# First layer's attention: the projections of heads 2 to 7 as seven products per head pair, with their sums on VectorE

## What is computed

```python
ql, kl, vl, ... = in_proj_split(h_l @ w_in)      # 256 latent tokens
qc, kc, vc, ... = in_proj_split(h_c @ w_in)      # 256 context tokens
# per head: q, k are 2 x 64 wide, v is 128 wide; rope on the latent q, k
def diff_attend(q, k, v, lam):
    s = jnp.einsum('bqhcd,bkhcd->bchqk', q, k).astype(jnp.float32) * (ATT_HEAD_DIM ** -0.5)
    p = jax.nn.softmax(s, axis=-1)
    a = p[:, 0] - lam * p[:, 1]
    return jnp.einsum('bhqk,bkhe->bqhe', a.astype(v.dtype), v)
o_l = diff_attend(ql, concat(kl, kc), concat(vl, vc), lam)
o_c = diff_attend(qc, kc, vc, lam)               # first layer only
```

## Time and profile before

| | us |
|---|---|
| median of 3 runs | 2659.3 |
| lowest, highest | 2656.21, 2660.04 |
| span of the profiled execution | 2653.7 |
| TensorE busy | 2620.1 (99%) |
| VectorE, ScalarE, GpSimd busy | 1544.2, 780.3, 1083.9 |

### The profile page before, as it was taken

One profiled execution on the slowest core, in us unless ns is written; L12 is line 12 of the kernel. 1 busy time (PEld: TensorE's weight loads), 2 busy tenths in 40 slices (PEclk: granted clock), 3 DMA queues, 4 the chain that ended last, 5 costly groups with the idle time before them and its releaser, 6 DMA issues.

```text
span 2653.7 us, 39393 instructions
## 1 busy us (share of the span) xinstructions
PE 2620.1 (99%) x15122; PEld 2004.0 (76%) x15122; DVE 1544.2 (58%) x2600; ACT 780.3 (29%) x1786; POOL 1083.9 (41%) x874
## 2 busy tenths in 40 slices
PE   8999999999999999999999999999999999999998
PEld 7779994555555666788878888876666677899998
DVE  1537835777778334797859760226766733566253
ACT  2430113565665333100021110013554522201210
POOL 4018971232323112274425554411221222586885
PEclk9999999999999999999999999999999999999999
DMA  9337666434432220244455532264444321287653
GB/s 284 97 112 213 180 200 168 111 96 106 106 99 72 56 54 26 72 113 129 123 159 160 162 91 88 87 183 117 111 108 107 96 72 50 79 224 216 172 167 120
DMA packets 519018, 330.96 MB, mean 125 GB/s; under 512 B 15296, under 2 KB 485680, under 8 KB 518832
## 3 DMA queue, kind: packets, MB, share of 16 engines
q1 hardware_dynamic: 507600, 296.10, 39.6%
q0 software_dynamic: 10784, 31.46, 4.8%
q10 hardware_dynamic: 448, 0.89, 0.1%
HBM read 327.06 MB, written 1.34 MB: 124 GB/s over the span
## 4 chain that ended last, share of the span: by engine, by line
PE 90%; DVE 3%; issue 2%; ACT 1%; DVEq 1%; POOL 1%; PEld 1%; PEldq 0%; DMA 0%; POOLq 0%; ACTq 0%
PE ps L1736 42%; PE ps L1373 23%; PE ps L1903 3%; PE ps L1915 3%; PE ps L1894 3%; PE ps L1878 2%; PE ps L1855 1%; PE ps L2017 1%; PE ps L2053 1%; PE ps L2040 1%; PE ps L2116 1%; POOL TMP L844 1%; PE ps L1693 1%; PE ps L2029 0%; PE ps L1841 0%
## 5 line engine op out<-in xcount | busy, mean ns | idle before, releaser
L1373 PE MATMUL ps<-xnT,W 128*128 128x512 f32 (+1 forms) x1760 | 650.2, 525 | 2.2 <-DVE TMP L2583 0.8
L1373 PEld LDWEIGHTS ps<-xnT,W 128*128 128x128 f32 x1760 | 329.8, 190 | 290.3 <-issue 260.1
L1736 PE MATMUL ps<-TMP,W 128*128 128x128 f32 (+1 forms) x2840 | 481.9, 320 | 3.6 <-DVE TMP L2450 2.8
L1736 PEld LDWEIGHTS ps<-TMP,W 128*128 128x128 f32 x2840 | 422.5, 192 | 35.9 <-issue 3.7
L1736 PE MATMUL ps<-BIG,W 128*128 128x128 f32 (+1 forms) x2744 | 438.6, 314 | 0.0
L819 POOL TENSOR_TENSOR W<-W 128x512 f32<-128x512 f32 x137 | 188.8, 1378 | 560.6 <-DMA W<-in_w_mlp 246.0
L1736 PEld LDWEIGHTS ps<-BIG,W 128*128 128x128 f32 x2744 | 393.1, 191 | 27.5 <-issue 1.2
L1736 PE MATMUL ps<-xnT,W 128*128 128x128 f32 (+1 forms) x2032 | 324.2, 311 | 0.0
L1736 PEld LDWEIGHTS ps<-xnT,W 128*128 128x128 f32 x2032 | 288.7, 191 | 18.9 <-issue 0.8
L905 ACT ACTIVATE TMP<-ps 128x512 f32<-128x512 f32 (+3 forms) x229 | 104.9, 465 | 653.5 <-PE ps L1736 394.5
L2208 DVE SCALAR_TENSOR_TENSOR TMP<-W,cact,TMP 128x512 f32<-128x512 f32 x168 | 205.8, 1258 | 7.9
(11 more groups left out here) (349 smaller groups left out, 3139.9 us busy)
## 6 DMA issues: line engine op xcount, KB each, us to landing
W<-in_w_in SPq DMA_DIRECT2D x188, 512.0 KB, 4.1
W<-in_w_mlp SPq DMA_DIRECT2D x128, 512.0 KB, 4.0
W<-in_ada_w SPq DMA_DIRECT2D x96, 512.0 KB, 4.0
BIG<-cs_rows POOLq DMA_DIRECT2D x96, 256.0 KB, 4.7
W<-in_w_ssd_o SPq DMA_DIRECT2D x32, 512.0 KB, 5.1
W<-in_w_gate SPq DMA_DIRECT2D x22, 512.0 KB, 6.1
W<-in_w_up SPq DMA_DIRECT2D x22, 512.0 KB, 4.5
W<-in_w_down SPq DMA_DIRECT2D x16, 512.0 KB, 3.6
```

Source lines behind the costliest of these rows:

```text
L1373: last = mm(dst, w[:, c, 0:m], rhs(k), start=k == 0, stop=k == total - 1)
L1736: done = mm(PS[bank][:, third + half * H:third + half * H + H], w[:, at + c, :], x[:, c, :], start=first and opens and c == 0, stop=last a ...
```

## The change

Heads 0 and 1 stay as they are. Heads 2 to 7 of the first layer are taken in three pairs, and each of q, k, v of a pair is a *job* (nine in all). A job multiplies the two heads' weights (two blocks of output columns), split in halves of the depth (4 chunks each), with the tokens, split by depth and by latent and context (256 each). This is a 2 x 2 by 2 x 2 block product, and it is done in seven block products (steps 1 to 7) in place of eight. Its sums are:

- of tokens, t1 to t4, once, by VectorE in units 0 to 3 (1024 elements each);
- of weights, four additions of 128x512 per job by VectorE, into two extra slots of the ring (`attsums`), spread over units 1 to 20 by the table `WEIGHT_SUMS`;
- of results: step 1 opens bank 4 and ScalarE copies it; steps 6, 7 and 4 add onto the same bank, and ScalarE copies after each (256 columns). Bank 5 takes step 2, is opened again by step 5, and step 3 adds onto it; VectorE adds bank 5 to the copied blocks after steps 2, 7 and 3. Each next step on a bank waits for that copy or addition.

A step is 4 matmuls of 256 columns (q, k) or 8 of 128 (v). `SEVEN_FILL` places the 63 steps in the slots of units 4 to 24; `GATE_FILL` places 12 gate matmuls in units 24 to 31. ScalarE makes the copy of part 0 ahead of the unit's exponentials if part 0 has exactly one step, and behind them otherwise. The token sums for the merge move to units 25 to 28. Odd pairs keep q, k and v in `qkB`, `vaB0`, `vaB1`, in space that the attention's output uses later. Rope of head 2 in unit 7 needs all four copies of the key job.

```diff
+SEVEN_JOBS = [(0, p, t) for p in (1, 2, 3) for t in "qkv"]
+SEVEN_AT = {1: 4, 2: 8, 3: 16}
+SEVEN_FILL[1] = [["q1 q2", "q6 q5", "q7"], ["q4 q3", "k1 k2", "k6 k5"], ["k7", "", "k4 k3"], ["v1 v2", "v6 v5", "v7"],
+                 ["v4 v3", "", ""]]
+SEVEN_FILL[2] = [["", "q1", "q2"], ["q6", "q5", "q7"], ["", "q4", "q3"], ["k1", "k2", "k6"], ["k5", "k7", ""],
+                 ["k4", "k3", "v1"], ["v2", "v6", "v5"], ["v7", "", "v4"], ["v3", "", ""]]
+SEVEN_FILL[3] = SEVEN_FILL[2]
+GATE_FILL = {24: (0, 1, 0), 25: (1, 1, 0), 26: (1, 1, 0), 27: (1, 0, 0), 28: (1, 1, 0), 29: (1, 0, 0), 30: (1, 1, 0),
+             31: (1, 0, 0)}
+WEIGHT_SUMS = {s: n for s, n in enumerate((0, 1, 1, 2, 2, 1, 2, 2, 1, 1, 2, 1, 1, 1, 1, 1, 1, 1, 2, 1, 2))}
...
+                def seven_copied(s, part):
+                    for job, step in seven_of(s, part) if l == 0 else ():
+                        if step in (1, 6, 7, 4):
+                            seven_done(act, job, step)
...
+                            A(seven_out(job, i, m), PS[4][:, 0:S], ACT.Copy, scale=scale).then_inc(c_cp, 1)
...
                 for s, (h, qt, k0, nk) in enumerate(us):
                     b = 2 * (s % 2)
+                    one = l == 0 and len(seven_of(s, 0)) == 1
+                    if one:
+                        seven_copied(s, 0)
                     act.wait_ge(u_mx["att"], 32 * l + s + 1)
...
+                    if not one:
+                        seven_copied(s, 0)
                     if s:
                         prob_t(s - 1)
+                    seven_copied(s, 1)
...
+                    if step == 1:
...
+                            pe.wait_ge(c_cp, 4 * job)
...
+                    elif step == 2:
+                        if job:
+                            pe.wait_ge(c_ad, 3 * job)
...
+                    elif step == 6:
+                        pe.wait_ge(c_ws, job + 1)
+                        pe.wait_ge(c_t, 2)
+                        pe.wait_ge(c_cp, 4 * job + 1)
...
+                    elif step == 5:
+                        pe.wait_ge(c_ad, 3 * job + 1)
...
+                    elif step == 7:
+                        pe.wait_ge(c_t, 4)
+                        pe.wait_ge(c_cp, 4 * job + 2)
...
+                    elif step == 4:
+                        pe.wait_ge(c_cp, 4 * job + 3)
...
+                    else:
+                        pe.wait_ge(c_ad, 3 * job + 2)
...
                     for n, t in enumerate(("ga", "gs")):
-                        pe.wait_ge(kept["att"], 24 * l + 24)
...
+                            pe.wait_ge(c_cp, 4 * len(SEVEN_JOBS))
+                            pe.wait_ge(c_ad, 3 * len(SEVEN_JOBS))
...
+                    if s:
+                        seven_added(s - 1, 2)
                     if h < 7 and qt == nq - 1 and l == 0:
+                        dve.drain()
                         rope(h + 1)
...
+                    seven_added(s, 0)
+                    seven_added(s, 1)
                     if s:
                         out_of(s - 1)
+                    if l == 0 and s < 4:
+                        next(seven_sums, None)
+                    for _ in range(WEIGHT_SUMS.get(s, 0) if l == 0 else 0):
+                        next(seven_weights, None)
-                    if (4 if l else 20) <= s < (16 if l else 24):
+                    if (4 if l else 25) <= s < (16 if l else 29):
                         next(first_token_sums, None)
```

More of the change, by code:

```diff
@@ L522, in build @@
         va = [va0, va1]
+        qkB, vaB0, vaB1 = carve(BIG[:, 8192:], (2, 2, T), (4, P), (4, P))
         fr, = carve(TMP[:, 1536:], (4, T))
@@ L595, in build @@
         out_t, out_d = sem("out_transposed"), sem("out_stored")
+        c_pe, c_cp, c_ad, c_ws, c_t = (
+            sem(f"seven_{x}") for x in ("products", "copied", "added", "weights_summed", "tokens_summed"))
         q_s, q_v, q_t, q_p1, q_p2, q_p7, q_rel = (
@@ L654, in slot_of, with weights_ready @@
             return W[:, number[key] % SLOTS, :, :]
-        def quick_weights(eng, j):
-            *pair, k1, k2 = quick_keys(j)
+        def weights_ready(eng, keys):
+            *pair, k1, k2 = keys
             for key in pair:
@@ L696, in flat, with seven_keys, paired, job_for @@
             return v.rearrange("p a b -> p (a b)")
+        def seven_keys(job):
+            l, p, t = SEVEN_JOBS[job]
+            return [("att", l, 2 * p, t), ("att", l, 2 * p + 1, t), ("attsums", l, p, t, 0), ("attsums", l, p, t, 1)]
+        def paired(l, h):
+            return l == 0 and h >= 2
+        def job_for(h, t):
+            return SEVEN_JOBS.index((0, h // 2, t))
+        def qk_of(l, h):
+            return (qkB if paired(l, h) and h // 2 % 2 else qk)[:, h % 2, :, :]
+        def va_of(l, h):
+            return ((vaB0, vaB1) if paired(l, h) and h // 2 % 2 else va)[h % 2]
+        def seven_done(eng, job, step):
+            if step in (1, 2, 7):
+                eng.wait_ge(c_pe, 3 * job + (1, 2, 7).index(step) + 1)
+            else:
+                made(eng, seven_keys(job)[{6: 0, 4: 1, 5: 2, 3: 3}[step]])
+        def seven_out(job, i, m):
+            l, p, t = SEVEN_JOBS[job]
+            whole = flat(va_of(l, 2 * p + i)) if t == "v" else qk_of(l, 2 * p + i)[:, "qk".index(t), :]
+            return whole[:, m * S:(m + 1) * S]
         def by_half(v):
@@ new lines, in _, with filled @@
+                many = 12 // (3 * nq)
+                def filled(s, part):
+                    h = us[s][0]
+                    if l == 0 and h:
+                        for job, step in seven_of(s, part):
+                            product_of(job, step)
+                        n = GATE_FILL.get(s, (0, 0, 0))[part]
+                    else:
+                        n = many if h < 7 else (8 // nq, 4 // nq, 0)[part]
+                    for _ in range(n):
+                        next(ahead, None)
@@ L2059, in _ @@
                 for s, (h, qt, k0, nk) in enumerate(us):
-                    if qt == 0:
+                    if qt == 0 and (l or h == 0):
                         ahead = pieces(h + 1) if h < 7 else gate_pieces(0)
+                    if l == 0 and s == min(GATE_FILL):
+                        ahead = gate_pieces(0)
                     scores(s)
-                    for _ in range(many if h < 7 else 8 // nq):
-                        next(ahead, None)
+                    filled(s, 0)
                     if s:
@@ new lines, in _, with seven_added @@
+                seven_sums, seven_weights = sums_for_seven(), weights_for_seven()
+                def seven_added(s, part):
+                    for job, step in seven_of(s, part) if l == 0 else ():
+                        if step not in (2, 7, 3):
+                            continue
+                        seven_done(dve, job, step)
+                        dve.wait_ge(c_cp, 4 * job + {2: 1, 7: 3, 3: 2}[step])
+                        i, m = {2: (0, 0), 7: (1, 1), 3: (0, 1)}[step]
+                        part_of = PS[5][:, 0:S]
+                        whole = seven_out(job, i, m)
+                        if SEVEN_JOBS[job][2] == "q":
+                            V.scalar_tensor_tensor(out=whole, in0=part_of, scalar=HD ** -0.5, in1=whole,
+                                                   op0=ALU.mult, op1=ALU.add).then_inc(c_ad, 1)
+                        else:
+                            V.tensor_tensor(whole, part_of, whole, ALU.add).then_inc(c_ad, 1)
```

142 lines of the change are left out of this document (112 added, 30 removed).

## The result

| | before | after |
|---|---|---|
| median, us | 2659.61 (4 runs) | 2673.64 (4 runs) |
| lowest, highest | 2656.21, 2660.04 | 2671.26, 2678.78 |
| span of the profiled execution | 2653.7 | 2669.5 |

The ratio is 1.006 (95% interval 1.0045 to 1.0074): slower by 14.0 us. The time lies inside the predicted range (2655 to 2674), and the direction is the forecast's, but +7.5 us were forecast, about half of what came. The profiled execution is the fastest of the four. The mechanism was right. What failed is one term that the prediction named and left out of its sum: GpSimd's instructions beside VectorE's.

A forecast was written before the change was run, and what follows sets the result against it. TensorE was taken as the bound in the first layer's attention. Unit stretches of 29.2, 148.7, 11 and 41.8 us gave 230.7, 7.5 more than before; added to the 2659.3 median: 2667 us, range 2655 to 2674.

The forecast's parts named there:

- Units 6, 15, 23: Lone product's copy precedes ScalarE's exponentials, nothing behind the transposes: TensorE waits 1.8 us each for values, 5.4 in all.
- Units 9, 10, 17, 18, 13, 21: Waits from lone q6 copies (9, 17: 0.5 us; 10, 18: 0.2) and weight sums delaying the maximum (13, 21: 0.6, 1.2).
- The rest of units 4 to 23: Scores, transposes, values, plus 42 products of 1.72 us and 20 of 1.79, without waits: 148.7 us.
- Upper side: GpSimd beside VectorE: GpSimd's rotations and merge sums slow VectorE, units 7, 16, 24 to 27: up to 5 us above the 7.5.
- Unit 7: Late key product, GpSimd's four rotations, rope and weights precede the addition that v5 waits for: 0.95 us.
- Unit 16: Product q2 waits for the addition of v3, which stands behind the probabilities: 0.4 us.
- Units 24 to 31: Pieces used up, so each unit lasts as long as its chain from scores to values: 41.8 us together.
- B: Rival: only bare chains count, VectorE keeps up, sums fall in gaps: 2658 us, at most 2664; chance 0.24.
- C: Rival: faster, values never wait as ScalarE's copy is done ahead of TensorE, thin units too: 2646 us; chance 0.10.
- D: Rival: each of the 63 products waits for its copy on the one bank, 38 us: 2682 us; chance 0.05.
- E: Rival: the change doesn't do what it says; built program shows 63 products for 72 pieces; chance 0.01.
- Too low if: Sign that the forecast is too low: single waits over 2 us at products 5 and 3 behind VectorE's additions.

The follow-up runs named there:

- e1_fill: Changed kernel with product 7 moved from behind scores to the empty slot behind the transposes in units 6, 15, 23: 2672.22 us, ratio 1.0048 to before.
- e4_rot_ws: Changed kernel with GpSimd's rotations of heads 3 and 5 held back and VectorE's weight sums begun one unit earlier: 2671.64 us, ratio 1.0044 to before.
- e11_no_rot: Changed kernel with first-layer rotations of heads 1 to 7 cut to 8 of 256 columns and GpSimd's merge sums held back: 2663.88 us, 1.0021 to before.
- e7_two: Changed kernel with only heads 2 to 5 by seven products, heads 6 and 7 by eight pieces as before: 2657.49 us, ratio 1.0000 to before.
- e9_busy: Changed kernel with 47 extra matmuls, results never read, put where TensorE waits: 2671.94 us, ratio 1.0053 to before.
- e5_all: Changed kernel with product 7 later, merge sums and two rotations held back, tail copies ahead of exponentials, weight sums earlier: 2658.80 us, 1.0003 to before.
- e8_two_fixed: Changed kernel with two pairs by seven, product 7 later, head 3's rotation held back, weight sums begun in unit 0: 2651.51 us, 0.9974 to before.

## Why the prediction was right or wrong

The stretches of the sum, forecast against the first trace of after:

| | forecast | measured |
|---|---|---|
| units 0 to 3 | 29.2 | 30.75 |
| units 4 to 23, waits | 11 | 12.7 |
| units 4 to 23, the rest | 148.7 | 149.2 |
| units 24 to 31 | 41.8 | 45.35 |
| sum, from 223.2 before | 230.7 (+7.5) | 238.0 (+14.8) |

**How a wait is counted.** The prediction counts from start to start; the waits view lists the idle time only. A wait costs 0.26 us more from start to start than the view lists. Rows usually overlap by 0.16, and that overlap is lost, and the row behind a wait is 0.1 longer. In unit 6 the values start 2.04 us behind the transposes where 0.44 is usual, so 1.60, and last 0.1 longer: 1.70 for a listed 1.44. The view also leaves out short waits. Unit 9, first a product, then ScalarE's copy, then TensorE's values:

```profile
935.66 1.89 PE L2169 MATMUL ps<-BIG,W 128*128 128x256 f32 x8
...
937.03 0.60 ACT L972 ACTIVATE TMP<-ps 128x512 f32<-128x512 f32 x1
...
937.69 1.16 PE L2130 MATMUL ps<-BIG,TMP 128*128 128x128 f32 x8
938.68 1.89 PE L2169 MATMUL ps<-BIG,W 128*128 128x256 f32 x8
```

Nothing is listed, but the values start 0.06 behind the end of the copy, 2.03 behind the product in place of 1.73: they waited 0.3, and 0.1 more stands in their own length (0.99 to the next start; the values of unit 6 before took 0.89). In units 4 to 23 there are 12 waits, eight listed (9.2 us) and four not (0.3): with 0.26 each, 12.7 us from start to start.

**Units 6, 15, 23.** Right: 1.70 each for the 1.8 forecast, for the reason named; e1_fill took them away. There the values still start 0.04 to 0.06 behind the copy.

**Units 9, 10, 17, 18, 13, 21.** Nearly right: 0.4, 0.3, 0.4, 0.3, 0.4 and 1.2 for 0.5, 0.2, 0.5, 0.2, 0.6 and 1.2. Unit 4 was too dear: 0.9 were forecast, and no wait is listed there.

**The rest of units 4 to 23.** Right to 0.5 us, and with it the price of a product. Where TensorE does not wait, a product behind the transposes takes 1.73 (1006.50 to 1008.23 in unit 19) and one beside scores 1.82 or 1.83, as pieces did (1.72, 1.82). TensorE's busy time fell by 9 us, not by the 15.7 that were forecast, though nine pieces are gone: at a wait the overlap of rows is lost and the next row is longer. An estimate from the 0.26 above is 5.2 us for 20 waits in the stage (16 listed, four not), and the lower clock adds 1.4, about the 6 that are missing.

**The step that failed: "Upper side: GpSimd beside VectorE".** The prediction saw the mechanism and named units 7, 16 and 24 to 27, but put none of it into the sum, and gave it at most 5 us. What the units took in its place:

- Unit 7: given 0.95, took 2.93 from start to start. In e4_rot_ws, with the rotation still in the chain but not beside VectorE, it waits 0.57 listed, 0.83 in all: the 0.95 was right without the collision, which cost 2.1.
- Unit 16: given 0.4, took two waits of 0.48 and 0.67 listed, and is 1.3 shorter in e4_rot_ws and e11_no_rot.
- Units 0 to 3 were taken as unchanged. Two weight sums and a token sum meet the rotation of head 1 in unit 2 and push the maximum of unit 3 back: 1.35, gone in e11_no_rot.
- Unit 24 took 8.35 for 7.2 and unit 29 8.19 for 6.3. With the merge sums held back they are 1.25 and 1.3 shorter.

Together 7.3 us, by the lengths of the units, and that is what the stage is longer than the sum (238.0 for 230.7). That the two are equal is luck: the lower clock of units 29 and 30 in this trace (1.4, below) is also not in the sum, and terms that were too dear, as unit 4's, cancel it. By the medians the kernel without GpSimd's rotations and merge sums stands 9.2 lower. Its +5.6 is near the +7.5 of the sum that left the term out, but by another way: the sum holds the rotation's length, and the run does not. The term was of the sum, not a tail: the rotation of each head starts by the end of the rope before it, so it falls on the same instructions in every run (v5 waits 2.66 or 2.67 us in six traces of five kernels). It belongs in the sum whenever the order of the program fixes the meeting. The page of the Trainium skill that the prediction cited (SBUF — State Buffer, "Who interferes with whom") says that a VectorE instruction with two SBUF inputs contends with a GpSimd instruction that reads SBUF. The weight sums (0.69 to 1.75) and probabilities (0.48 to 1.50) agree, and so does the addition that reads PSUM (0.41 in both); the 128x1 factor is held as well (0.22 to 1.29).

**Units 24 to 31.** Right where GpSimd is not: 5.51, 5.06, 4.40, 5.43 for the forecast 5.5, 5, 4.4, 5.7. Bare chains are long: e7_two shows the loss is the third pair's. Unit 30 took 5.04 for 4.1, all of it by the lower clock: it takes 4.13 in e9_busy.

**The clock.** Not in the sum at all: 0 to 2 us in the median. In the first trace of the changed kernel it is 1.4 us of the stage, which took 236.6 in e9_busy.

**The rivals.** B (2658, VectorE keeps up, only bare chains count) is about what e5_all reached once the collisions and ScalarE's order were mended, so it described a kernel that this change was not. C (values never wait) fell: 13 waits. D (every product waits for its copy) fell: the view lists two waits at a product, both behind VectorE, not behind ScalarE's copy (e4_rot_ws, e5_all and e8_two_fixed have one of 0.2 behind a copy, in unit 4). The Trainium skill (Perfetto Trace Analysis, "Matmuls") asks that independent groups rotate through the banks. Here the alternation of 4 and 5 with other work between was enough. E did not occur.

**"Too low if".** The last sentence of the prediction, waits of over 2 us at products 5 and 3 behind VectorE's additions, is in part what came: 2.67 at v5, and 3.55, of which 2.5 were in the sum, at the gate product behind v3's addition. At a product 3 no wait is listed.

## What to carry to other kernels

- Removing TensorE work pays only while enough of it is left beside a chain. Here the first two pairs are worth 6 us once their places are mended, and the third costs 7: count what each unit's chain needs as cover and stop there.
- When work is moved to an engine with free time, look at which single instructions it will stand in front of, and which engine shares its memory at that moment. Leaving out 25 us of sums gained 1 to 2 us; taking GpSimd's rotations and merge sums away some 9.
- If the order of the program fixes a collision, price it in the sum, not in the range.
